# Product-key choices placed in thirteen slots of a turn, and some of them up to a head sooner, in a one-core decoder step

## The reference, cut to what matters

```python
q = (xb @ w_q).reshape(blk, PEER_HEADS, 2, half)       # 8 heads, two halves of 128
q = (q - mu) * lax.rsqrt(var + LN_EPS)
s = jnp.einsum('thpd,hpnd->thpn', q, keys_f)           # 2 x 128 scores
s1, i1 = lax.top_k(s[:, :, 0], 16)
s2, i2 = lax.top_k(s[:, :, 1], 16)
cand = (s1[..., :, None] + s2[..., None, :])           # 256 candidates
sc, ci = lax.top_k(cand, 16)
idx = e1 * 128 + e2                                    # 16 experts a token and head
gate = jax.nn.softmax(sc, axis=-1)
h = jax.nn.gelu(jnp.einsum('thkd,td->thk', u_tab[idx], xb))
y = jnp.einsum('thk,thkd->td', gate * h, v_tab[idx])
```

## Time and profile before

| | |
|---|---|
| median of 3 runs | 1952.78 us (1948.48 to 1953.85) |
| the profiled execution | 1945.02 us, span of its records 1943.3 us |
| granted TensorE clock, mean | 0.837 of full speed |
| TensorE busy | 1425.5 us, 73% of the span |
| VectorE busy | 1166.8 us, 60% |
| GpSimd busy | 988.5 us, 51% |
| ScalarE busy | 402.3 us, 21% |
| DMA | 675.82 MB, mean 348 GB/s over the span |
| of it the gathers of GpSimd | 545.33 MB |
| the chain that ended last | TensorE 38%, DMA 28%, VectorE 17%, GpSimd 9%, issue 6% |

### The profile page before, as it was taken

How to read it: one execution, slowest core, us unless ns; L and a number is a source line. 1 busy time by engine, 2 the same in 40 slices (tenths; PEclk the granted TensorE clock), 3 DMA queues, 4 the chain that set the end, 5 groups by cost and what they waited for, 6 DMA issues and landing times.

```text
span 1943.3 us, 19827 instructions
## 1 busy us (share of the span) xinstructions
PE 1425.5 (73%) x6736; PEld 894.8 (46%) x6736; DVE 1166.8 (60%) x2987; ACT 402.3 (21%) x819; POOL 988.5 (51%) x1052
## 2 busy tenths in 40 slices
PE   8999998798977879989894995354733346674565
PEld 7888887675553456556561553022401011230113
DVE  1110113887677566676678765877878867866511
ACT  2320201242341221232111221111321211211010
POOL 0000000446664546565565765776767776767761
PEclk9999999898997889998997998777866655687778
DMA  7336541799999999999999999999999999999993
GB/s 275 128 133 237 193 155 40 263 386 384 408 411 372 394 384 408 412 411 411 409 403 399 392 410 412 410 408 400 407 370 409 404 407 364 404 374 407 408 381 126
DMA packets 172597, 675.82 MB, mean 348 GB/s; under 512 B 19497, under 2 KB 22697, under 8 KB 158674
## 3 DMA queue, kind: packets, MB, share of 16 engines
q0 software_dynamic: 149760, 545.33, 71.4%
q1 hardware_dynamic: 22738, 129.23, 17.4%
HBM read 667.07 MB, written 7.41 MB: 347 GB/s over the span
## 4 chain that ended last, share of the span: by engine, by line
PE 38%; DMA 28%; DVE 17%; POOL 9%; issue 6%; ACT 1%; SPq 0%; DVEq 0%; POOLq 0%; PEldq 0%; ACTq 0%
DMA at<-in_v_tab,idxV 16%; PE PJ L1445 14%; DMA at<-in_u_tab,idx 8%; PE Y L1495 7%; DVE at L1215 6%; POOL at L679 5%; PE PJ L1343 5%; PE PJ L1327 4%; POOL at L670 4%; PE PJ L1350 3%; DMA at<-in_state 2%; PE PJ L1404 1%; DMA out_st_s<-at 1%; DVE at L1143 1%; DVE at L1081 1%
## 5 line engine op out<-in xcount | busy, mean ns | idle before, releaser
L670 POOL DMA_INDIRECT at<-in_u_tab,idx x512 | 487.9, 953 | 610.7 <-DVEq L1198 342.2
L1215 DVE CUSTOM_DVE_ANT_0 at<-at,XD 128x1024 f32<-128x1024 f32 x512 | 616.0, 1216 | 232.0 <-DMA at<-in_u_tab,idx 220.2
L1495 PE MATMUL Y<-at,at 128*32 128x512 f32 x2048 | 357.9, 824 | 394.8 <-DMA at<-in_v_tab,idxV 394.8
L679 POOL DMA_INDIRECT at<-in_v_tab,idxV x512 | 483.9, 945 | 298.2 <-PE Y L1495 167.5
L1445 PE MATMUL PJ<-at,at 128*128 128x256 f32 (+1 forms) x1792 | 414.1, 391 | 4.4 <-issue 1.7
L1445 PEld LDWEIGHTS PJ<-at,at 128*128 128x128 f32 x1792 | 343.2, 194 | 77.8 <-issue 20.5
L1495 PEld LDWEIGHTS Y<-at,at 128*32 128x32 f32 x2048 | 74.8, 134 | 591.0 <-issue 589.0
L1343 PE MATMUL PJ<-at,at 128*128 128x256 f32 (+2 forms) x960 | 224.1, 393 | 6.2 <-DVE at L1122 5.4
L1343 PEld LDWEIGHTS PJ<-at,at 128*128 128x128 f32 (+2 forms) x960 | 170.1, 180 | 62.8 <-issue 14.3
L1327 PE MATMUL PJ<-at,at 128*128 128x256 f32 (+1 forms) x640 | 143.5, 383 | 0.0
L1327 PEld LDWEIGHTS PJ<-at,at 128*128 128x128 f32 (+1 forms) x640 | 108.7, 171 | 40.6 <-issue 14.3
(11 more groups left out here) (208 smaller groups left out, 1271.6 us busy)
## 6 DMA issues: line engine op xcount, KB each, us to landing
at<-in_w_blk SPq DMA_DIRECT2D x72, 1024.0 KB, 7.4
at<-in_w_q SPq DMA_DIRECT2D x16, 1024.0 KB, 8.0
at<-in_w_o SPq DMA_DIRECT2D x8, 1024.0 KB, 7.1
at<-in_u_tab,idx POOLq DMA_INDIRECT x512, 11.4
at<-in_v_tab,idxV POOLq DMA_INDIRECT x512, 11.3
at<-in_state SPq DMA_DIRECT2D x4, 1024.0 KB, 8.4
out_st_s<-at SPq DMA_DIRECT2D x4, 1024.0 KB, 6.6
at<-in_w_pg SPq DMA_DIRECT2D x2, 2048.0 KB, 13.6
```

The source lines that it names most:

```text
L670: pool.indirect_dma_start(ubuf[slot], None, u_tab, bass.IndirectOffsetOnAxis(rows_of, 0)).then_inc(u_in[slot], 16)
L679: pool.indirect_dma_start(vbuf[slot], None, v_tab, bass.IndirectOffsetOnAxis(rows_of, 0)).then_inc(v_in[slot], 16)
L1215: v.tensor_tensor_reduce(out=t, in0=t, in1=XD[:, :], scale=1.0, scalar=0.0, op0=ALU.mult, op1=ALU.add, accum_out=hraw[:, n % 2, k:k + 1]). ...
L1495: last = mm(Y[32 * c:32 * c + 32, s, :], wpadV[d // PAIR % 2][:, g, :], vbuf[slot][:, 512 * s:512 * s + 512], start=False, stop=final)
```

## The change

Only the placing of choices in `choices_at()` changes. The slots within a choice become 0, 2, 5, 7, 9, 10, 11, 12 and 13. Heads 3, 4, 17, 18 and 27 to 31 still begin in slot 0 of turn r-3 and now end in slot 13 of that turn. Heads 5 to 9 and 19 to 21 follow one another 13 slots apart and so begin up to one turn sooner: head 5 in slot 13 of turn 1 instead of slot 0 of turn 2, head 9 in slot 1 of turn 5 instead of slot 0 of turn 6. Heads 10 to 15 begin in slot 0 of turn r-4, a whole turn sooner. The dense choices, head 16 and heads 0 to 2 stay.

```diff
@@ choices_at()
         elif r == 2 * PH:
             put(choice(*divmod(r, PH)), r - 3, (7, 9, 11, 13, 15, 16, 17, 19, 21))
         else:
-            put(choice(*divmod(r, PH)), r - 3, (0, 2, 6, 10, 13, 14, 16, 18, 20))
+            first = max(TOPK * (r - 4), 13 * (r - 4) + TOPK if r < 2 * PH else 13 * (r - 2 * PH) + TOPK * 13 + 7)
+            first = min(first, TOPK * (r - 3)) if r <= SAMPLE_ROUTES_AT + 2 else TOPK * (r - 3)
+            put(choice(*divmod(r, PH)), 0, [first + k for k in (0, 2, 5, 7, 9, 10, 11, 12, 13)])
```

## The result

The changed kernel takes 1954.29 us at the median of 20 runs (1948.86 to 1963.67). In the same series the kernel before takes 1949.51 us (20 runs, 1946.59 to 1953.85). The ratio is 1.0027 with a 95% interval of 1.0018 to 1.0036, so the change costs 5.3 us (3.5 to 7.0; the two medians by themselves are 4.8 apart), where 3.5 us less had been forecast. Run again in two later series it came to 1.0029 (1.0016 to 1.0042) and 1.0027 (1.0015 to 1.0039). The kernel is slower in all three, by just under the 0.3% that a single comparison can tell.

A forecast was written before the change was run, and what follows sets the result against it. The gather stream bounds the kernel, six thin stretches losing 26.3 us. Terms -3 - 2 - 3 + 2 + 2 + 0.5 + 0 = -3.5 us from 1952.8 give 1949.3 us, own range 1941 to 1956, wider range 1937 to 1963.

The forecast's parts named there:

- 700 to 725: Sample states in turn 5: choice parts before the last update add 4.1 us to the last state product; +2 (0 to +5.5).
- cover of 7 us: Full gather stream: some 7.0 us of gathers queued on the DMA engines, so VectorE may be that late without loss.
- 1635 to 1660: Turn 26, sample dots: head 28's choice now ends before the turn; -2 of the 6.0 us lost (-5 to +3).
- 1720 to 1755: Turn 27: head 30's choice now fills VectorE's waits for products; -3 of the 4.6 us lost (-4.6 to +1).
- 1065 to 1090: Last `x1` norm: head 15's choice leaves, so norm, weights and transposes come up to 7 us sooner; -3 (-3.6 to 0).
- Turn 16: Norm of `x2` of tile 0 among head 19's parts: dots 9.6 us late, 2.6 beyond the cover; +2 (0 to +5).
- The scores: Packed choices: part 2 waits a few tenths for the scores' copy in each of 23 choices; +0.5 us (0 to +5).
- The three more table loads of ScalarE: 146 loads against 143, 1283 ns each, 3.9 us on an engine busy 21%; taken as 0 (0 to +3.9).
- VectorE's wait for the norm: After the last sample state's product: this wait was to grow beyond 4.49 us, a sign of being right.
- The packed choices that stand alone: Compressed choices away from other work: VectorE 4.2 us late, costed at nothing because queued gathers keep running.
- The second rival: Turns from 6 on: late dots delay v gathers and open four new holes, +14.9 us, 1967.7 us; chance 0.20.
- a choice's index: GpSimd's gathers: no choice after the first is late, and GpSimd still never waits for one after the change.

The follow-up runs named there:

- g3_packed: Against the kernel before: general-rule heads get the new packed slots but start in slot 0 of turn r-3 as before; 1.0025, +4.9 us.
- f3_late: Against the kernel before: only heads 17 to 21 and 27 to 31 have the new places; 1.0003, +0.6 us.
- h3_only_head9_packed: Against the kernel before, on a slower chip: heads start as in the changed kernel with the old wide slots, only head 9 packed; 1.0015 (0.9990 to 1.0041).
- e2_late: Against the kernel before, on a slower chip: only heads 17 to 21 and 27 to 31 have the new places; 1.0002 (0.9970 to 1.0033).
- h2_late_but_two: Against the kernel before, on a slower chip: only heads 17 to 21 and 27 to 29 have the new places; 1.0024 (0.9991 to 1.0057).
- k1_only_head9_packed: Against the kernel before: all heads start as in the changed kernel with the old wide slots, only head 9 packed; 1.0019, +3.7 us.

## Why the prediction was wrong

**Two steps failed**, and both had the stream's slack wrong. The first is the term for 700 to 725, "TensorE has other jobs, and the stream has its 7 us; I take +2". The 4.1 us on the way to the last state product was exactly right (7.4 became 11.5). What it is worth was mis-sized: 690 to 740 loses 6.0 us more than before. Two things stood wrong in the judgement. TensorE has no other job there: the sums stand behind the state product in its order, and the v gathers behind the sums. And the cover of 7 us was not free: before, the same v gather was already late. These are the first and the last of its rows before.

```profile
678.77 0.94 POOL L679 DMA_INDIRECT at<-in_v_tab,idxV  x1 [0.31 <-issue]
...
694.78 0.94 POOL L679 DMA_INDIRECT at<-in_v_tab,idxV  x1 [5.09 <-PE Y L1495]
```

Three pairs lie between them, as after, so it is 694.78 - 678.77 - 7.7 = 8.3 us late, with 0.7 lost. Of the further 15.1 - 8.3 = 6.8 us, 6.0 were lost. (4.1 of the 6.8 are the pieces of the choice, 2.3 the later arrival of the state, on which the prediction had no term.) The size of the cover itself was well estimated: 15.1 late lost 6.7, 13.3 lost 6.5, 8.2 lost 0.5 and 8.3 lost 0.7, which makes 8.4, 6.8, 7.7 and 7.6 us; `g3_packed` alone (12.4 late, 2.7 lost) makes 9.7. The sum had 7.0, and 8.2 was worked out from the Trainium skill, DMA: Bandwidth & Descriptors, section Anatomy of one DMA; these traces don't tell the two apart.

**The gains** are the second step, and by the windows the larger one. The sum had -3 - 2 - 3 = -8 us for three holes; they gave 0 - 4.1 + 3.4 = -0.7. With 6.0 in place of the +2 alone it would have come to +0.5; the missing gains are another 7.3. 1635 to 1660 was taken as -2 and gave -4.1 (1630 to 1700). 1720 to 1755 was taken as -3: VectorE's wait for a product of 3.42 us is indeed gone, but 1700 to 1800 loses 3.4 more. That a filled wait shortens the stream was argued and is false here. `f3_late` says the same in time: +0.6 us where the terms of the turns from 16 on add up to -3. What makes the new loss was not found; 374 to 384 GB/s stand there in the eleven traces (those of the two slower chips aside) in which heads from 17 on are packed or start sooner, 391 and 392 in the two with the old order. 1065 to 1090 was taken as -3: it improved from 351 to 385 GB/s, but 1060 to 1130 as a whole is 389 in both, so the hole moved to 1110 and 0 remains.

**The small terms.** Turn 16, taken as +2, cost little: the dots stood at 1232.48 to 1254.36, 21.9 us for what was worked out as 22.4, but 1130 to 1420 moved 407 instead of 408 GB/s, 0.7 us, and no thin place came at 1245. Here 21.9 - 12.8 = 9.1 us late fitted under the cover nearly for nothing. The scores, +0.5: VectorE's wait for their copy rose from 4.6 to 8.7 us in all, over the 8 that was set; one wait of 5.33 us stands in turn 5, at 674.71 in front of the last state, where VectorE then waited 4.60 instead of 11.01 for the state anyway. The three more table loads of ScalarE came (146 against 143), 3.9 us on an engine busy 21%. These rows of ScalarE, between the last state's product and the square root of its norm, show how closely two loads follow each other.

```profile
709.44 1.28 ACT L820 ACT_TABLE_LOAD   x1
710.73 0.20 ACT L820 ACTIVATE sdR<-mvR 128x2 f32<-128x2 f32 x1
710.95 1.28 ACT L901 ACT_TABLE_LOAD   x1
```

Each of them costs its 1.28 us and the next instruction follows within 0.02. The drain of about 1.38 us that the Trainium skill, ScalarE: Activation LUTs, section What ACT_TABLE_LOAD costs, adds isn't visible here. VectorE's wait for the norm, 4.49 us before, grew to 5.08.

**In sum**, by windows: 0 - 4.1 + 3.4 + 0.8 + 6.0 + 0.7 = 6.8, and 1.1 more from 600 to 690 (381 and 376 GB/s), makes 7.9 us. From the first gather to the last the two profiled executions take 1902.02 - 344.55 = 1557.5 and 1913.10 - 347.97 = 1565.1 us, 7.7 more. Their spans differ by 9.5, because the first gather already came 3.4 us later, at a point up to which both kernels have the same order: that part isn't the change's. The series measured 5.3. One execution differs from another by some us at the same place: 690 to 740 moves 332, 331 and 326 GB/s in three executions of the changed kernel. The packed choices that stand alone were costed at nothing, and where no other chain meets them that held: 740 to 1060 moves 410 GB/s in both. The second rival had the right kind of mechanism (late dots, then late v gathers, then a dry stream), but in one place that was known to be late, not in four new ones. GpSimd did wait for a choice's index, 3.78 us at 1289.51 and 1.43 at 510.99, against what was set down; 1285 to 1295 moved 402 GB/s, so the longer one cost 0.2 us.

**Luck.** The measured 1954.29 lies within the 1941 to 1956 that the forecast gave itself, but only because it started from 1952.8, the median of three runs; over 20 runs the kernel before takes 1949.51. The direction was wrong.

**Not settled:** why the store ahead of the last state took longer, what gives back at 1700 to 1800 the gain of 1635, and by which of its many small holes the packed kernel without sooner starts loses 4.9 us.

## What to carry to other kernels

A cover of queued transfers may be spent once: before a delay is written off against it, count how late the same queue already is at that place; what went beyond was lost nearly in full here. A gain in one thin stretch is not yet a gain in time: look at the next 100 us as well, where it may be given back. Follow a moved instruction through every in-order queue behind it (here VectorE's update, TensorE's product and sums, GpSimd's gather), not to its own consumer alone. Fill idle time of an engine only where the thing waited for doesn't come in several pieces: what stands between the pieces of a chain lengthens it by its full duration, however idle the engine was just before.

## What the runs showed of the hardware

On two chips, those of the first and the fourth series, the kernel before took 2052.79 and 2048.59 us; in the other series 1947.5 to 1949.5. The stream of gathers is slower there, above all in later turns: `h3_only_head9_packed` moves 408 GB/s from 740 to 1060 us, as elsewhere, but `e2_late` and `h2_late_but_two` move only 374 from 400 to 600 already, where `f3_late` has 395. These are two later windows of `h3_only_head9_packed`.

```profile
1470.00:1630.00 160.00, 54.64 (x266) 14.38 (x266) 117.42 (x319) 31.80 (x61) 104.38 (x111) 0.61 0.96 367
1700.00:1800.00 100.00, 63.45 (x222) 28.86 (x226) 65.68 (x175) 17.77 (x35) 60.79 (x65) 0.64 0.91 337
```

The same kernel (`k1_only_head9_packed`) elsewhere moves 406 and 375 GB/s in them. In the first the share of the DMA engines' time fell from 1.02 to 0.96, 6%, and the bytes by 10%: the engines were busy a little less and also moved some 4% less per busy time. Why was not looked into. The Trainium skill, HBM Reference, section Specifications (TRN2), says that a core streaming alone gets more than its share of some 358 GB/s and falls to about that when its neighbour streams too; 367 lies near that and 337 below it, the 408 GB/s at 740 to 1060 would not fit without more, and no run here shows what the neighbour did. A difference of 0.3% can't be measured there.
